# Turning the state-space scans back: two tiles in one set of GpSimd operations

## The chip, the cores and the metric

One core of a Trainium2 chip runs the whole kernel. The metric is the device time of one execution in microseconds (us). The kernel before takes 1242.14 us (median of three runs, 1241.8 to 1242.48). The engines are called PE (TensorE), DVE (VectorE), ACT (ScalarE), POOL (GpSimd) and SP (SyncE, which only issues the transfers here).

## The reference, cut to what matters

Two layers of a decoder trunk on 256 positions of width 1024. Each layer is a gated feed-forward, then four token mixers side by side (stick-breaking attention, an S5 state-space mixer, gated linear attention, dilated attention), gates and an output projection, then a second feed-forward. The change lies in the S5 mixer:

```python
lam_bar = jnp.exp(lam * dt)                                   # complex, one per state
bu = jnp.einsum('bsgh,gph->bsgp', uf.astype(jnp.complex64), b_bar)
def combine(e1, e2):
    a1, b1 = e1
    a2, b2 = e2
    return a1 * a2, a2 * b1 + b2
_, states = lax.associative_scan(combine, (a, bu), axis=1)    # s[t] = lam_bar * s[t-1] + bu[t]
y = jnp.einsum('bsgp,ghp->bsgh', states, c_mat).real + d_skip * uf
```

## The kernel before, in words

PE does all the matrix products in float32r. Every weight block (128 partitions by 2048 columns) is split into a high and a low part, and each product is three matmuls (or a wide one and a correction): ACT writes the high part (`w_hi`, L869), DVE writes the rest (`w_lo`, L1163, two operations of 1024 columns a block). The blocks run through a ring of three slots, filled by SP.

The mixer stage of a layer is a list of 31 blocks, `SEQ`; block number `m` is a projection, a gate or a branch output. Each engine has its own program for the stage, written out by hand: for every `m`, PE multiplies the block and then runs `pieces(m)`; DVE evacuates the block's bank (`evacuate`, L1604; some blocks are evacuated by ACT), splits a later block (`rest_of_weights`, L1163) and then runs its own `pieces(m)`; ACT does the like. Within an engine the order is fixed, and an operation that waits holds up all behind it. Between engines there are only counting semaphores.

The S5 mixer has 1024 complex states, 8 tiles of 128 partitions, handled as four pairs of tiles. The complex recurrence is made real by turning the input by tables of cosines and sines (`rotC`, `rotS`, in tile `G`), scanning with a real decay, and turning the result back. For pair `p`, with `S5_AT = (1, 5, 9, 13)`:

- at m = `S5_AT[p]` PE multiplies the input (`s5_in`), and DVE turns it (`s5_rotate`, L1387 to L1392) into `s5x`;
- at m one later DVE scans (`s5_scan`, L1399, four scans of 256 columns);
- POOL then turns back (`s5_pair`, L1753 to L1766) from `s5x` into `st`: for each of the two tiles six operations of 256 columns: four products, then the two sums. It is all that POOL does at that time. The second to last and last operations of a tile wait for the products, as POOL waits for its own semaphore through `own.link` and `tt` (L1664);
- five blocks after `S5_AT[p]` PE multiplies `st` by the output matrix (`s5_out`, L653). `s5_state` counts one for each tile; its readers wait for the pair's second (L655, L1383, L1597).

Of DVE's other work near it, the change's surroundings hold `rest_of_weights` (L1163: reads `raw` and `w_hi`), the stick-breaking weights of heads 2 and 3 at m = 11 (L1447: reads `attA` and the constant `strict`), and the softmax scores of the dilated attention at m = 16 (L1411 to L1414). At m = 12 PE waits for `sb_w`, which the last L1447 of m = 11 raises, before it multiplies `sbv` by `attA`:

```python
if m == 12:
    pe.wait_ge(s.gla_zread, layer * PER.gla_zread + 1)
    pe.wait_ge(s.sb_w, layer * PER.sb_w + HEADS)
    pe.wait_ge(s.evac_a, layer * PER.evac_a + NTH[SLOT["sbv"]])
    attend(2, sbv, attA).then_inc(s.sb_o, 1)
    gla_scores(1)
```

At m = 20 PE's product waits until DVE has evacuated block 18 (L1604, two blocks before, the same bank).

After the mixers POOL adds the four branches (`mix`, L1768): an operation of 512 columns (L1664 on `attA` or `attB`) and one of 256 (L1773) for each of eight tiles; this part is not changed.

Of the kernel before, what the change touches and what calls it, by code (L numbers as in the profile page):

```python
# [11 lines left out]
ALU = mybir.AluOpType  # L12
AX = mybir.AxisListType

P = 128
LAYERS = 2
T = 256
# [89 lines left out]
class PER:  # L107
# [87 lines left out]
    m_lo = 8  # L195
    dve = 63
    act = 13
    pool = 232


class Signals:
# [29 lines left out]
def build(nc, x_in, stream, params_in, const_in, out):  # L231
    ctx = ExitStack()
    with ctx:
        def sb(name, shape, dt=F32):
            return ctx.enter_context(nc.sbuf_tensor(name, shape, dt))
# [22 lines left out]
        st = sb("st", [P, 2, 2, T])  # L258
# [17 lines left out]
        rotC, rotS = G[:, 2, :, :], G[:, 3, :, :]  # L276
# [30 lines left out]
        s = Signals()  # L307
# [1349 lines left out]
        def _(pool):  # L1657
            pool.memset(attB[:, 0, 0:T], 0.0).then_inc(s.warm, 1)
            pool.wait_ge(s_const, 16)
            for layer in range(LAYERS):  # L1660
                own = Steps(pool, s.pool, layer, PER.pool)

                def tt(o, a, b, op):
                    own.link(pool.tensor_tensor(o, a, b, op))  # L1664
# [88 lines left out]
                def s5_pair(pair):  # L1753
                    x = s5x
                    pool.wait_ge(s.s5_scan, layer * PER.s5_scan + pair + 1)
                    if pair >= 1:
                        pool.wait_ge(s.s5_y, layer * PER.s5_y + pair)
                    for i in range(2):
                        t = 2 * pair + i
                        own.mark(pool.tensor_tensor(x[:, i, 0, 0, :], x[:, i, 1, 0, :], rotC[:, t, :], ALU.mult))  # L1760
                        own.mark(pool.tensor_tensor(x[:, i, 0, 1, :], x[:, i, 1, 1, :], rotC[:, t, :], ALU.mult))
                        re, im = st[:, i, 0, :], st[:, i, 1, :]
                        own.mark(pool.tensor_tensor(re, x[:, i, 1, 1, :], rotS[:, t, :], ALU.mult))
                        own.link(pool.tensor_tensor(im, x[:, i, 1, 0, :], rotS[:, t, :], ALU.mult))
                        tt(re, x[:, i, 0, 0, :], re, ALU.subtract)
                        pool.tensor_tensor(im, x[:, i, 0, 1, :], im, ALU.add).then_inc(s.s5_state, 1)  # L1766

                def mix(dt):  # L1768

# [10 lines left out]
                for pair in range(ST // 2):  # L1780
                    s5_pair(pair)
# [140 lines left out]
```

## Time and profile before

| | |
|---|---|
| Time, median of three | 1242.14 us |
| Time of the profiled execution | 1242.35 us |
| Its span | 1240.6 us |
| PE busy | 1231.1 us (99%) |
| DVE busy | 944.0 us (76%) |
| ACT busy | 677.7 us (55%) |
| POOL busy | 369.1 us (30%) |
| Granted TensorE clock | 1.0 of full speed in the mixer stages |

The span is what lies between the first and the last recorded instruction. Busy is the sum of the recorded durations, overlaps counted once. A recorded duration of a DVE or POOL operation includes the time in which it was issued but held up, so the same operation can show two lengths. Each layer's mixer stage runs from about 205 to 440 us in layer 0 and 614.3 us later in layer 1, with the same pattern.

### The profile page before, as it was taken

What the parts mean: (1) busy time and instruction counts of PE and PEld (TensorE: products, weight loads), DVE (VectorE), ACT (ScalarE), POOL (GpSimd) and SP (SyncE); (2) the same over time, 40 slices, a digit from 0 to 9 for tenths busy, and PEclk for the clock granted to TensorE, in tenths of its full rate; (3) what the DMA queues carried; (4) which work ended last, traced back from release to release, by engine and by line L of the source; (5) the groups of instructions that cost most, each with busy time, mean ns of one, the idle gap of its engine ahead of it and who ended that gap; (6) DMA issues with size and microseconds to landing.
All of it is one profiled execution on the core that took longest, in us unless ns stands there. A gap on an engine that the chain in (4) does not pass through costs nothing.

```text
span 1240.6 us, 23671 instructions
## 1 busy us (share of the span) xinstructions
PE 1231.1 (99%) x9190; PEld 1154.5 (93%) x9190; DVE 944.0 (76%) x1241; ACT 677.7 (55%) x999; POOL 369.1 (30%) x511
## 2 busy tenths in 40 slices
PE   8999999999999999999999999999999999999998
PEld 8999989999999999999999999999999999999998
DVE  6767788889887876666776778788997788666765
ACT  5666645773653554545556655558645445454553
POOL 0088990344404200000001889704443041000000
PEclk9999999999999999999999999999999999999999
DMA  8554554533344465455545454554433445555441
GB/s 333 216 197 160 185 181 179 184 139 134 137 169 172 170 246 193 177 179 193 174 170 199 173 199 173 182 188 170 136 137 137 170 170 204 192 182 190 171 181 68
DMA packets 31605, 220.44 MB, mean 178 GB/s; under 512 B 3633, under 2 KB 3761, under 8 KB 5425
## 3 DMA queue, kind: packets, MB, share of 16 engines
q1 hardware_dynamic: 31536, 219.49, 49.6%
q8 instruction: 48, 0.79, 0.2%
q14 instruction: 21, 0.16, 0.0%
HBM read 218.42 MB, written 1.05 MB: 177 GB/s over the span
## 4 chain that ended last, share of the span: by engine, by line
PE 94%; DVE 3%; ACT 1%; issue 1%; DMA 1%; SPq 0%; DVEq 0%; ACTq 0%
PE banks L520 21%; PE banks L478 20%; PE banks L479 19%; PE banks L480 19%; PE banks L522 10%; PE banks L491 5%; DVE w_lo_t L1163 1%; DVE u_t L1177 1%; DVE hT L1348 1%; ACT w_hi_t L869 1%; DMA raw<-weights 1%; DVE sbqk L1280 0%; DVE sbqk L1278 0%; PE banks L714 0%; DVE w_lo_t L1196 0%
## 5 line engine op out<-in xcount | busy, mean ns | idle before, releaser
L1163 DVE TENSOR_TENSOR w_lo_t<-raw,w_hi_t 128x1024 fp32r<-128x1024 f32 x400 | 507.2, 1308 | 100.1 <-ACT w_hi_t L869 99.6
L869 ACT ACTIVATE w_hi_t<-raw 128x1024 fp32r<-128x1024 f32 x400 | 399.4, 1046 | 115.7 <-PE banks L480 114.4
L478 PE MATMUL banks<-u_t,w_hi_t 128*128 128x256 f32 x944 | 271.5, 288 | 4.1 <-DVE w_lo_t L1196 2.5
L479 PE MATMUL banks<-u_t,w_hi_t 128*128 128x256 f32 x944 | 267.0, 283 | 0.0
L480 PE MATMUL banks<-u_t,w_lo_t 128*128 128x256 f32 x944 | 266.9, 283 | 0.0
L520 PE MATMUL banks<-u_t,w_hi_t 128*128 128x512 f32 x576 | 204.0, 398 | 0.0
L520 PE MATMUL banks<-b_t,w_hi_t 128*128 128x512 f32 x576 | 204.0, 398 | 0.0
L478 PEld LDWEIGHTS banks<-u_t,w_hi_t 128*128 128x128 f32 x944 | 180.8, 191 | 11.5 <-DVE w_lo_t L1196 3.5
L479 PE MATMUL banks<-h_lo_t,w_hi_t 128*128 128x256 f32 x672 | 190.2, 283 | 0.0
L480 PE MATMUL banks<-h_hi_t,w_lo_t 128*128 128x256 f32 x672 | 190.1, 283 | 0.0
L478 PE MATMUL banks<-h_hi_t,w_hi_t 128*128 128x256 f32 x672 | 190.1, 283 | 0.0
L479 PEld LDWEIGHTS banks<-u_t,w_hi_t 128*128 128x128 f32 x944 | 180.9, 192 | 0.1
L480 PEld LDWEIGHTS banks<-u_t,w_lo_t 128*128 128x128 f32 x944 | 180.8, 192 | 0.0
L522 PE MATMUL banks<-u_t,w_lo_t 128*128 128x256 f32 x576 | 161.8, 281 | 0.0
L522 PE MATMUL banks<-b_t,w_lo_t 128*128 128x256 f32 x576 | 161.8, 281 | 0.0
L520 PEld LDWEIGHTS banks<-b_t,w_hi_t 128*128 128x128 f32 x576 | 108.2, 188 | 25.8
L520 PEld LDWEIGHTS banks<-u_t,w_hi_t 128*128 128x128 f32 x576 | 108.2, 188 | 25.8
L478 PEld LDWEIGHTS banks<-h_hi_t,w_hi_t 128*128 128x128 f32 x672 | 128.5, 191 | 1.8
L480 PEld LDWEIGHTS banks<-h_hi_t,w_lo_t 128*128 128x128 f32 x672 | 128.7, 191 | 0.0
L479 PEld LDWEIGHTS banks<-h_lo_t,w_hi_t 128*128 128x128 f32 x672 | 128.6, 191 | 0.0
L924 ACT ACTIVATE sbqk<-sbqk 128x256 f32<-128x256 f32 x88 | 36.8, 418 | 165.6 <-DVE sbqk L1280 120.4
L522 PEld LDWEIGHTS banks<-u_t,w_lo_t 128*128 128x128 f32 x576 | 108.9, 189 | 0.0
(234 smaller groups left out, 1998.0 us busy)
## 6 DMA issues: line engine op xcount, KB each, us to landing
raw<-weights SPq DMA_DIRECT2D x202, 1024.0 KB, 4.9
raw<-weights SPq DMA_DIRECT2D x3, 512.0 KB, 8.3
prm<-params SPq DMA_DIRECT2D x1, 1178.5 KB, 5.3
prm<-params SPq DMA_DIRECT2D x1, 1166.5 KB, 10.1
out_t<-hT SPq DMA_DIRECT2D x4, 256.0 KB, 2.2
cst<-constants SPq DMA_DIRECT2D x1, 896.0 KB, 9.7
hT<-x_t SPq DMA_DIRECT2D x2, 256.0 KB, 3.8
raw<-weights SPq DMA_DIRECT2D x2, 256.0 KB, 4.0
```

Of the source, the lines that this page charges most:

```text
L478: pe.matmul(o, st[0], mv[0], start=start, stop=False, skip_group_check=True)
L479: pe.matmul(o, st[0], mv[1], start=False, stop=False, skip_group_check=True)
L480: ins = pe.matmul(o, st[1], mv[0], start=False, stop=stop, skip_group_check=True)
L491: return pe.matmul(o, st, mv, start=start, stop=stop, skip_group_check=True)
L520: pe.matmul(banks[:, bank + ct, :], st[0], in_t[where][:, :, kt, :], start=kt == 0, stop=False, skip_group_check=True)
L522: ins = pe.matmul(banks[:, bank + ct, 0:T], st[1], in_hi[where][:, kt, :], start=False, stop=kt == KT - 1, skip_group_check=True)
L869: act.activation(w_hi[:, slot, a:a + HALF], raw[:, slot, a:a + HALF], ACT.Copy) \
L924: act.activation(ab[:, buf, 0, :], ab[:, buf, 0, :], ACT.Silu).then_inc(s.h_silu, 1)
L1163: dve.tensor_tensor(w_lo[:, slot, a:a + HALF], raw[:, slot, a:a + HALF], w_hi[:, slot, a:a + HALF].bitcast(F32), ALU.subtract) \
L1177: ins = dve.scalar_tensor_tensor(out=in_lo[where][:, kt, :], in0=hT[:, kt, :], scalar=p_(name)[:, kt:kt + 1], in1=in_hi[where][:, kt, :].b ...
L1348: dve.scalar_tensor_tensor(out=hT[:, 2 * q:2 * q + 2, :].rearrange("p a t -> p (a t)"), in0=banks[:, q, :], scalar=0.5, in1=hT[:, 2 * q:2 ...
```

## The change

POOL turns both tiles of a pair with the same operations. The first one multiplies real and imaginary parts of both tiles by the cosines (1024 columns, the cosine table repeated over the two parts), two of 512 columns multiply by the sines, and two of 512 columns make the sums. The number of own steps that POOL counts falls from 232 to 204. The first sum no longer counts as an own step but raises `s5_state`, and so does the second, so the counter still stands at two more after each pair.

```diff
-    pool = 232
+    pool = 204
...
-                    for i in range(2):
-                        t = 2 * pair + i
-                        own.mark(pool.tensor_tensor(x[:, i, 0, 0, :], x[:, i, 1, 0, :], rotC[:, t, :], ALU.mult))
-                        own.mark(pool.tensor_tensor(x[:, i, 0, 1, :], x[:, i, 1, 1, :], rotC[:, t, :], ALU.mult))
-                        re, im = st[:, i, 0, :], st[:, i, 1, :]
-                        own.mark(pool.tensor_tensor(re, x[:, i, 1, 1, :], rotS[:, t, :], ALU.mult))
-                        own.link(pool.tensor_tensor(im, x[:, i, 1, 0, :], rotS[:, t, :], ALU.mult))
-                        tt(re, x[:, i, 0, 0, :], re, ALU.subtract)
-                        pool.tensor_tensor(im, x[:, i, 0, 1, :], im, ALU.add).then_inc(s.s5_state, 1)
+                    two = slice(2 * pair, 2 * pair + 2)
+                    cos = rotC[:, two, :].unsqueeze(2).to_broadcast([P, 2, 2, T])
+                    sin = rotS[:, two, :]
+                    own.mark(pool.tensor_tensor(x[:, :, 0, :, :], x[:, :, 1, :, :], cos, ALU.mult))
+                    re, im = st[:, :, 0, :], st[:, :, 1, :]
+                    own.mark(pool.tensor_tensor(re, x[:, :, 1, 1, :], sin, ALU.mult))
+                    own.link(pool.tensor_tensor(im, x[:, :, 1, 0, :], sin, ALU.mult))
+                    pool.tensor_tensor(re, x[:, :, 0, 0, :], re, ALU.subtract).then_inc(s.s5_state, 1)
+                    pool.tensor_tensor(im, x[:, :, 0, 1, :], im, ALU.add).then_inc(s.s5_state, 1)
```

## Rows read from the trace of the kernel before

**Rows 1.** The page: busy time of PE and POOL; the chain that ended last, by engine.
```profile
PE 1231.1 (99%) x9190; PEld 1154.5 (93%) x9190; DVE 944.0 (76%) x1241; ACT 677.7 (55%) x999; POOL 369.1 (30%) x511
...
PE 94%; DVE 3%; ACT 1%; issue 1%; DMA 1%; SPq 0%; DVEq 0%; ACTq 0%
```
**Rows 2.** Timeline of POOL in pair 2: start us, us, engine, line, operation.
```profile
282.43 1.71 POOL L1760 TENSOR_TENSOR s5x<-s5x,G 128x256 f32<-128x256 f32 x1 [15.70 <-DVE s5x L1399]
284.10 1.71 POOL L1761 TENSOR_TENSOR s5x<-s5x,G 128x256 f32<-128x256 f32 x1
285.78 1.05 POOL L1763 TENSOR_TENSOR st<-s5x,G 128x256 f32<-128x256 f32 x1
```
**Rows 3.** Timeline of DVE beside it, the two L1163 and L1447 apart.
```profile
282.31 1.23 DVE L1163 TENSOR_TENSOR w_lo_t<-raw,w_hi_t 128x1024 fp32r<-128x1024 f32 x1
283.46 1.76 DVE L1163 TENSOR_TENSOR w_lo_t<-raw,w_hi_t 128x1024 fp32r<-128x1024 f32 x1
285.14 1.09 DVE L1447 SCALAR_TENSOR_TENSOR attA<-attA,cst 128x384 f32<-128x384 f32 x1
286.16 1.09 DVE L1447 SCALAR_TENSOR_TENSOR attA<-attA,cst 128x384 f32<-128x384 f32 x1
```
**Rows 4.** Timeline of PE: end of blocks 10 and 12, start of `pieces(12)`.
```profile
265.75 0.38 PE L478 MATMUL banks<-u_t,w_hi_t 128*128 128x256 f32 x1
271.69 1.06 PE L491 MATMUL banks<-st,s5c 128*32 128x256 f32 x8
...
281.41 0.38 PE L478 MATMUL banks<-u_t,w_hi_t 128*128 128x256 f32 x1
287.35 1.57 PE L491 MATMUL banks<-attA,sbv 128*64 128x256 f32 x16
```
**Rows 5.** POOL in the branch sums (L1768): 512 columns alone and beside L1163.
```profile
374.85 1.29 POOL L1664 TENSOR_TENSOR attA<-attA 128x512 f32<-128x512 f32 x1 [47.94 <-DVE attA L1578]
...
389.81 2.21 POOL L1664 TENSOR_TENSOR attA<-attA 128x512 f32<-128x512 f32 x1 [5.73 <-DVE attA L1578]
```
**Rows 6.** DVE beside the last row of Rows 5.
```profile
389.65 1.22 DVE L1163 TENSOR_TENSOR w_lo_t<-raw,w_hi_t 128x1024 fp32r<-128x1024 f32 x1
390.78 2.32 DVE L1163 TENSOR_TENSOR w_lo_t<-raw,w_hi_t 128x1024 fp32r<-128x1024 f32 x1
```
**Rows 7.** DVE in pair 1, and an unhindered operation of L1447's size.
```profile
249.37 0.56 DVE L1442 TENSOR_TENSOR attA<-attA,cst 128x384 f32<-128x384 f32 x1
...
253.83 3.09 DVE L1163 TENSOR_TENSOR w_lo_t<-raw,w_hi_t 128x1024 fp32r<-128x1024 f32 x2
259.82 3.47 DVE L1163 TENSOR_TENSOR w_lo_t<-raw,w_hi_t 128x1024 fp32r<-128x1024 f32 x2 [2.90 <-ACT w_hi_t L869]
263.22 2.10 DVE L1447 SCALAR_TENSOR_TENSOR attA<-attA,cst 128x384 f32<-128x384 f32 x2
```
**Rows 8.** POOL in pair 1, first and last of twelve.
```profile
253.41 0.74 POOL L1760 TENSOR_TENSOR s5x<-s5x,G 128x256 f32<-128x256 f32 x1 [14.48 <-DVE s5x L1399]
...
265.98 0.74 POOL L1766 TENSOR_TENSOR st<-s5x,st 128x256 f32<-128x256 f32 x1
```
**Rows 9.** POOL's first operation of pair 3; DVE beside and after pair 3.
```profile
314.11 0.74 POOL L1760 TENSOR_TENSOR s5x<-s5x,G 128x256 f32<-128x256 f32 x1 [18.22 <-DVE s5x L1399]
...
319.74 0.69 DVE L1604 SCALAR_TENSOR_TENSOR G<-banks,rstd_row 128x512 f32<-128x512 f32 x1 [1.53 <-PE banks L480]
320.89 3.10 DVE L1163 TENSOR_TENSOR w_lo_t<-raw,w_hi_t 128x1024 fp32r<-128x1024 f32 x2 [0.46 <-ACT w_hi_t L869]
339.36 0.68 DVE L1604 SCALAR_TENSOR_TENSOR G<-banks,rstd_row 128x512 f32<-128x512 f32 x1
```
**Rows 10.** Timeline of PE: the start of block 20.
```profile
340.67 0.36 PE L478 MATMUL banks<-u_t,w_hi_t 128*128 128x256 f32 x1
```
**Rows 11.** Layer 1: L1447's second operation, and PE's `pieces(12)`.
```profile
900.47 1.09 DVE L1447 SCALAR_TENSOR_TENSOR attA<-attA,cst 128x384 f32<-128x384 f32 x1
...
901.66 1.57 PE L491 MATMUL banks<-attA,sbv 128*64 128x256 f32 x16
```

## The prediction

> **What bounds the kernel now.** I read the page first: PE is busy 99% of the span and makes 94% of the chain that ended last; POOL is busy 30% [rows 1]. So a saving on POOL is worth nothing by itself, and the question is what else these operations touch. The list of waits, read next, has nobody waiting for POOL in the state-space part: the only entries of that part are POOL's own waits for DVE's scans, and PE shows no wait for an engine in the blocks after the first few of the stage beyond 0.4 us. What is left is the timelines of POOL and DVE laid side by side, and there both engines have operations of two lengths.
>
> POOL's 256-column operation takes 0.74 us [rows 8] or 1.71 us [rows 2]; the long ones lie beside DVE's split of weights (L1163). DVE's takes 1.23 us or 1.76 us [rows 3], and L1447 takes 1.09 us where an operation of its size takes 0.56 us [rows 3, 7]. In times: POOL's first operation of pair 2 is issued at 282.43 and ends at 284.14, that is 0.60 us after DVE's first L1163 has ended at 283.54; DVE's second is issued at 283.46 and ends at 285.22, 1.08 us after POOL's has ended; POOL's second ends at 285.81, 0.59 us after that [rows 2, 3]. So one of them works while the other stands, a whole instruction at a time, in turns. All DVE operations that show it read two tiles in SBUF; those that read a bank of PSUM and one tile do not.
>
> The Trainium skill has this as a rule: "SBUF — State Buffer", section "Who interferes with whom", says that a DVE instruction with two SBUF inputs and a GpSimd instruction that reads SBUF exclude each other, whoever is first holding the shared port for its whole instruction. By that rule the trace agrees (0.60 and 1.08 us after the other's end), and it speaks against this change, since it makes the holder's instruction longer. By that rule the sum would be the one worked out below; with turns taken within an instruction it would be nothing, the first rival.
>
> **Does the held time grow with the instruction?** The branch sums have a POOL operation of 512 columns: alone it takes 1.29 us, beside L1163 2.21 us [rows 5]. It ends at 392.02, 1.15 us after DVE's first L1163 (390.87), and DVE's second L1163 takes 2.32 us, ending 1.08 us after 392.02 [rows 6]. So POOL holds 0.60 us with 256 columns and 1.15 with 512, which is 0.55 us for each further 256; for 1024 columns I extend the line to 2.25 us. That length stands in no row. From below, it could let DVE in between its rows of 256 and hold no more than 0.60 us at a time; from above, four full operations of 0.74 are 2.96 us. I take 2.25, by the rows of 512.
>
> **The change part by part.** (1) POOL's own time for a pair. Before: twelve holds of 0.60 us, 7.2 us; after: 2.25 + 4 x 1.15 = 6.85 us. With the gaps, the pair gets about 1 to 2 us shorter (before, 253.41 to 266.72 in pair 1 [rows 8]). Nobody waits for it: worth 0. If the pair got longer instead, with every new operation held up as the worst old one (1.71 for 0.74, so 2.3 times some 7.5 us = 17 us), it would still just meet the first PE or DVE use, some 17 us after the start of a pair.
>
> (2) Semaphores: one wait of POOL on itself in a pair goes where there were four; `s5_state` reaches the same count at the last operation. Worth 0; its readers wait for the pair's second count.
>
> (3) What DVE stands for. Each POOL operation now stops a DVE operation for up to 1.15 or 2.25 us where it was 0.55. It costs where DVE is late. I looked for the blocks where DVE has no slack before PE. The tight one is m = 12: DVE's last L1447 ends at 287.25, and PE starts the product that needs it at 287.35, without a wait (block 12 took 5.94 us, as block 10 did) [rows 3, 4]. Slack 0.1 us. From 259.82, where DVE waits for ACT, to there DVE has no idle time, so a delay in it goes through. Layer 1 has the same 0.09 us (901.56 and 901.66) [rows 11].
>
> Pair 2, step by step, with the issue order of before (DVE's L1163 first at 282.31, POOL at 282.43). DVE's first L1163 to 283.54. POOL's 1024 columns: 283.54 + 2.25 = 285.79. DVE's second L1163: + 1.08 = 286.87. POOL's first 512: + 1.15 = 288.02. L1447, first: + 0.42 (as 286.23 from 285.81 in the rows' pattern, 0.56 less what overlaps) = 288.44. POOL's second 512: + 1.15 = 289.59. L1447, second: + 0.42 = 290.01. That is 2.76 us later than 287.25, and PE's `pieces(12)` starts 2.7 us late.
>
> (4) Pair 1 feeds the same chain. POOL starts at 253.41; its 1024 columns end at 255.66, DVE's first L1163 at 256.74, POOL 257.89, DVE 258.97, POOL's third 260.12; DVE's next L1163 (issued 259.82) ends at 261.20, POOL 262.35, DVE 263.43, POOL's fifth 264.58, L1447 265.00 and, now alone, 265.5. Before, they ended at 265.32 [rows 7]. About +0.2 us; pair 0 ends earlier and lets DVE start pair 1 up to 0.4 us earlier. From -0.3 to +0.5; I take 0.
>
> (5) Pair 3 lies beside the softmax of the dilated attention. POOL starts at 314.11 and DVE is 2.2 us late after its first L1163 pair there; the wait for PE before 319.74 (1.53 us) takes up most of it, and L1163 at 320.89 is issued some 0.3 us late [rows 9], just when POOL's third operation ends. If DVE is first, two further holds cost it about 0.5 us more than before; if POOL is first, about 1.7. What hangs on it is the evacuation of block 18, which ends at 340.04 with block 20 waiting for it at 340.67 [rows 9, 10]: slack 0.63. So 0 or about 1.1 us for a layer. DVE is issued some 0.1 us ahead by this count, so I take 0.
>
> (6) PE has no time to give back behind m = 12: what it waits there, the span grows by. Sum: 2 layers x 2.7 = 5.4 us on the profiled execution, whose span of 1240.6 us has 1.75 us around it that stay: 1242.35 + 5.4 = 1247.75. The median before is 0.2 us less than that execution; I say 1247.7.
>
> **The rivals.** *Nothing moves* (0.17): DVE is let in at least between the rows of 256 columns, so it stands for 0.55 us at a time as before, and pair 2 keeps its 287.25. Then POOL's saving is hidden and the time is 1242.1. For it: no row has 1024 columns or a table repeated over a dimension. Against it: the row of 512 with two rows of 256 in it, where DVE stood for 2.32 - 1.23 = 1.09 us.
>
> *Faster* (0.03): fewer holds, and the sum of them in a pair is 0.35 us less, so if POOL's longer operations fell on DVE's PSUM work, L1447 would end earlier. But PE has no wait there now to lose, so it could bring only the tenths of waits elsewhere, at most 1 us in all (1241). That is where it decides: only if the first operation of pair 2 ran clear of L1163.
>
> *More* (0.25): the tie in pair 3 goes to POOL, or the 1024 columns hold 2.96 us: 5.4 + 2 x 1.1 = 7.6, so 1249.9, or 5.4 + 2 x 0.7 = 6.8, so 1249.1.
>
> *Half of it* (0.10): the order at the start of pair 2 shifts by the 0.12 us that separate the two engines, or POOL's 512 columns find L1447's two operations already through, and only the 1024-column hold counts (2.25 - 0.60 = 1.65 us a layer): 1245.4.
>
> **How the numbers follow.** The forecast's own case has 0.45 and gives 1246.8 to 1248.6. The range of 1243.5 to 1250.6 takes in the larger and the half case and leaves out the hidden and the faster one. A measurement of this kernel can tell about 0.2%, 2.5 us, from no change: slower than 1244.6 has 0.45 + 0.25 + 0.10 = 0.80, within it 0.17, faster 0.03.
>
> **What would show it.** In the changed kernel's timeline the second L1163 of pair 2 should take about 3.4 us (1.76 before), L1447's two operations about 1.6 each (1.09), and PE should show a wait for DVE's `attA` at m = 12 of about 2.7 us, twice, at equal places of both layers. POOL's own sum of these lines should fall and its 1024-column operation should last 2.4 us where it runs alone. The rest of PE's waits stays. The forecast is wrong if no DVE operation is longer than the 2.32 us of before, or if DVE's late end at m = 12 is there but PE had slack that the rows hide.

## The result, and the profile after

| | before | changed |
|---|---|---|
| Median | 1242.16 us (4 runs, 1241.8 to 1242.48) | 1253.63 us (4 runs: 1252.35, 1252.41, 1254.86, 1255.11) |
| Profiled execution | 1242.35 us, span 1240.6 | 1252.41 us, span 1250.6 |
| Mean granted TensorE clock | 1.0 | 0.997 (0.994 to 0.995 in the two longer runs) |

The ratio of changed to before is 1.0091, with a 95% interval of 1.0079 to 1.0103: slower by 11.5 us, where 5.5 were forecast. The direction was right, the forecast size was half of what came, and the time lies outside the range.

The page, busy times and the chain by engine:

```profile
PE 1235.6 (99%) x9190; PEld 1158.5 (93%) x9190; DVE 964.4 (77%) x1241; ACT 677.5 (54%) x999; POOL 354.8 (28%) x455
...
PE 91%; DVE 5%; ACT 1%; issue 1%; DMA 1%; SPq 0%; ACTq 0%; DVEq 0%
```

Against [rows 1] POOL does its work in 14.3 us less, DVE is busy 20.4 us longer with the same instructions, and DVE has 5% of the chain. The groups of instructions say where: L1163 of DVE grew from a mean of 1308 to 1363 ns, L1447 from 1090 to 1360.

```profile
L1163 DVE TENSOR_TENSOR w_lo_t<-raw,w_hi_t 128x1024 fp32r<-128x1024 f32 x400 | 529.0, 1363 | 91.4 <-ACT w_hi_t L869 90.8
L1447 DVE SCALAR_TENSOR_TENSOR attA<-attA,cst 128x384 f32<-128x384 f32 x8 | 10.6, 1360 | 0.0
```

Pair 2 of layer 0, POOL's timeline (start, us):

```profile
282.36 3.41 POOL L1761 TENSOR_TENSOR s5x<-s5x,G 128x1024 f32<-128x1024 f32 x1 [17.96 <-DVE s5x L1399]
285.74 2.25 POOL L1763 TENSOR_TENSOR st<-s5x,G 128x512 f32<-128x512 f32 x1
287.95 1.58 POOL L1764 TENSOR_TENSOR st<-s5x,G 128x512 f32<-128x512 f32 x1
```

and DVE's beside it:

```profile
282.28 1.23 DVE L1163 TENSOR_TENSOR w_lo_t<-raw,w_hi_t 128x1024 fp32r<-128x1024 f32 x1
283.43 3.43 DVE L1163 TENSOR_TENSOR w_lo_t<-raw,w_hi_t 128x1024 fp32r<-128x1024 f32 x1
286.78 1.63 DVE L1447 SCALAR_TENSOR_TENSOR attA<-attA,cst 128x384 f32<-128x384 f32 x1
288.33 1.63 DVE L1447 SCALAR_TENSOR_TENSOR attA<-attA,cst 128x384 f32<-128x384 f32 x1
```

These answer to [rows 2] and [rows 3]. The two engines take turns, and each of POOL's turns has grown: its 1024 columns end 2.26 us after DVE's first L1163 (283.51 to 285.77), its 512 columns 1.13 us after the second (286.86 to 287.99). The second L1447 ends at 289.96, where before it ended at 287.25.

PE's timeline at m = 12 in layers 0 and 1, then at m = 17 in layer 0 (a number in brackets is PE's idle time ahead of the row):

```profile
290.06 1.63 PE L491 MATMUL banks<-attA,sbv 128*64 128x256 f32 x16 [2.67 <-issue]
...
910.87 1.54 PE L491 MATMUL banks<-attA,sbv 128*64 128x256 f32 x16 [2.66 <-issue]
...
332.18 1.64 PE L491 MATMUL banks<-dqk 64*128 64x128 f32 x8
```

The last row holds the matmuls of two heads and took 0.94 us before. It is longer because those of the second head start only at 332.93, after DVE's second L1414 has ended at 332.79.

The stretches after the first of these waits, each with its length, then PE's busy time, PEld, DVE, ACT, POOL, granted clock, DMA share and GB/s:

```profile
288.00:290.00 2.00, 0.00 (x0) 0.00 (x0) 2.00 (x3) 1.49 (x2) 1.92 (x2) 1.00 0.87 287
290.00:292.00 2.00, 1.95 (x24) 1.59 (x25) 2.00 (x2) 0.28 (x1) 2.00 (x2) 0.84 0.56 234
292.00:294.00 2.00, 2.00 (x46) 2.00 (x44) 2.00 (x2) 0.32 (x1) 1.29 (x1) 0.50 0.00 0
294.00:296.00 2.00, 2.00 (x28) 1.94 (x29) 0.98 (x3) 0.00 (x0) 0.00 (x0) 0.50 0.36 70
296.00:298.00 2.00, 2.00 (x11) 2.00 (x11) 2.00 (x5) 0.00 (x0) 0.00 (x0) 0.50 0.84 324
298.00:300.00 2.00, 2.00 (x18) 2.00 (x18) 1.83 (x6) 0.00 (x0) 0.00 (x0) 0.95 0.33 139
```

Here is what the forecast lacked. PE stands still through 288 to 290, works again from 290.06, and is then granted 0.50 of its clock (the 1.2 GHz level) from about 291.4 to 298.2. It looks busy, but block 13 comes late: the multiplication for pair 3 (`s5_in(3)`) starts at 302.45 where it was 296.71, and 3.03 of those 5.74 us arose after PE had resumed.

Following marks of PE's program through both profiles (start of the same group of matmuls, changed less before) gives the whole account in us; a row is what was added there:

| | layer 0 | layer 1 |
|---|---|---|
| m = 12, PE waits for L1447 | 2.73 | 2.73 |
| behind it, half clock | 3.03 | none (-0.04) |
| m = 17, PE waits for L1414 | 0.70 | 0.84 |
| all else in the layer | 0.0 | 0.0 |

The sum is 10.0, the growth of the span. The two longer executions took some 2.5 to 2.7 us more at a mean clock of 0.994 to 0.995. That fits a second stretch at half clock in layer 1, or a longer one in layer 0; they left no trace.

### The profile page after: what moved, and what is told of

Same layout as the page of the kernel before. It is cut to its first block, busy times and chain, and to the rows that moved or that the text cites. A ratio compares the mean times of both kernels' runs of the same rounds, so it can differ in the third digit from the quotient of the medians.

```text
span 1250.6 us, 23615 instructions
## 1 busy us (share of the span) xinstructions
PE 1235.6 (99%) x9190; PEld 1158.5 (93%) x9190; DVE 964.4 (77%) x1241; ACT 677.5 (54%) x999; POOL 354.8 (28%) x455
## 4 chain that ended last, share of the span: by engine, by line
PE 91%; DVE 5%; ACT 1%; issue 1%; DMA 1%; SPq 0%; ACTq 0%; DVEq 0%
PE banks L520 20%; PE banks L478 19%; PE banks L479 18%; PE banks L480 18%; PE banks L522 10%; PE banks L491 5%; DVE w_lo_t L1163 2%; ACT w_hi_t L869 1%; DVE u_t L1177 1%; DVE hT L1348 1%; DMA raw<-weights 1%; DVE sbqk L1280 0%; DVE sbqk L1278 0%; PE banks L714 0%; DVE w_lo_t L1196 0%
## 5 line engine op out<-in xcount | busy, mean ns | idle before, releaser
L1163 DVE TENSOR_TENSOR w_lo_t<-raw,w_hi_t 128x1024 fp32r<-128x1024 f32 x400 | 529.0, 1363 | 91.4 <-ACT w_hi_t L869 90.8
L478 PEld LDWEIGHTS banks<-u_t,w_hi_t 128*128 128x128 f32 x944 | 181.4, 192 | 11.5 <-DVE w_lo_t L1196 3.5
```

Of the source, the lines that this page charges most:

```text
L478: pe.matmul(o, st[0], mv[0], start=start, stop=False, skip_group_check=True)
L1163: dve.tensor_tensor(w_lo[:, slot, a:a + HALF], raw[:, slot, a:a + HALF], w_hi[:, slot, a:a + HALF].bitcast(F32), ALU.subtract) \
```

## The experiments

The theory before the experiments: POOL holds DVE off for a whole instruction; it costs time only where a late DVE operation is one that PE waits for; and the idle PE sometimes gets the lower clock afterwards. The rival: the wide form costs by itself, spread over the stage. The "before" of these runs had medians of 1242.3 to 1242.4 us.

**Wide in pair 2 alone, and wide in all but pair 2.** `s5_pair` chooses the form by pair:

```diff
+                    if pair in (2,):        # the other kernel: (0, 1, 3)
                         ...                 # the change's five operations
+                    else:
+                        ...                 # the twelve of before
```

> Only pair 2 of each layer is turned back in the wide form (one operation of 1024 columns, four of 512); pairs 0, 1 and 3 keep the twelve of 256. Theory (GpSimd holds DVE off for a whole instruction, and it matters only where DVE has no slack before PE, at m = 12; the idle PE then gets a lower clock for some 7 us in some executions): PE waits 2.7 us at m = 12 of each layer and not at m = 17, 1242.2 + 5.4 = 1247.6 us, and 3 us more for each layer in which the clock falls (up to 1253.6). Rival (the cost comes with each wide pair alike): a quarter of the change's 11.5 us, 1245.0 us, with waits spread over the stage.

Measured: 1249.18 us (1248.05 to 1249.94), ratio 1.0057 (1.0040 to 1.0074). In the profile, at clock 1.000, PE waits 2.66 us at m = 12 in each layer, its marks move by 2.73 there, and nothing is lost at m = 17:

```profile
290.65 1.11 PE L491 MATMUL banks<-attA,sbv 128*64 128x256 f32 x10 [2.66 <-issue]
```

The profiled execution took 1248.05 us; the two at a clock of 0.997 took 1249.9.

> Pairs 0, 1 and 3 wide, pair 2 in the old form. Theory: no wait of PE at m = 12, only the 0.7 to 0.8 us at m = 17 that pair 3 makes, in each layer: 1243.7 us, and the clock stays at 1.0. Rival (each wide pair costs alike): three quarters of 11.5 us, 1250.8 us.

Measured: 1243.0 us, ratio 1.0005 (0.9996 to 1.0015), clock 1.0. PE's marks move by 0.00 at m = 12 and by 0.42 and 0.43 at m = 17, less than the 0.7 to 0.8 that I expected: here DVE's L1163 of pair 3 was issued at 320.59, just ahead of POOL at 320.68, and its two operations took 3.45 us, where they took 3.81 in the change. One wide pair of four thus carries almost all of the loss, and three carry 0.7 us. The rival, that each costs alike, is out.

**The 1024 columns cut in two of 512.**

```diff
-                    cos = rotC[:, two, :].unsqueeze(2).to_broadcast([P, 2, 2, T])
                     ...
-                    own.mark(pool.tensor_tensor(x[:, :, 0, :, :], x[:, :, 1, :, :], cos, ALU.mult))
+                    for part in range(2):
+                        own.mark(pool.tensor_tensor(x[:, :, 0, part, :], x[:, :, 1, part, :], rotC[:, two, :], ALU.mult))
```

> The change with its operation of 1024 columns cut in two of 512 (real part of both tiles, imaginary part of both tiles), six operations a pair. Theory (held for the whole instruction, 1.15 us for 512 columns, 2.25 for 1024): DVE's second L1163 of pair 2 takes 2.3 us in place of 3.4, but one more GpSimd operation then comes ahead of L1447; its second ends 1.1 us earlier than in the change, PE waits 1.6 us at m = 12: about 1246.5 us, with up to 3 us a layer more if so short a wait also brings the clock down. Rival (the wide form as such is slow, or the clock falls whatever the wait's length): as the change, 1252 to 1254 us.

Measured: 1247.16 us (1247.05 to 1247.42), ratio 1.0039 (1.0025 to 1.0053), clock 1.0 in all five runs. PE's wait at m = 12:

```profile
288.59 1.54 PE L491 MATMUL banks<-attA,sbv 128*64 128x256 f32 x16 [1.57 <-issue]
```

The wait is 1.57 us, as counted in holds; at m = 17 the marks move by 0.96 us a layer. No clock was lost. With shorter instructions the cost falls to less than half of the change's 11.5 us: what costs is how long each instruction is.

**The 1024 columns third, not first.**

```diff
-                    own.mark(pool.tensor_tensor(x[:, :, 0, :, :], x[:, :, 1, :, :], cos, ALU.mult))
                     re, im = st[:, :, 0, :], st[:, :, 1, :]
                     own.mark(pool.tensor_tensor(re, x[:, :, 1, 1, :], sin, ALU.mult))
-                    own.link(pool.tensor_tensor(im, x[:, :, 1, 0, :], sin, ALU.mult))
+                    own.mark(pool.tensor_tensor(im, x[:, :, 1, 0, :], sin, ALU.mult))
+                    own.link(pool.tensor_tensor(x[:, :, 0, :, :], x[:, :, 1, :, :], cos, ALU.mult))
```

> The change with its operation of 1024 columns third among the five in place of first. Theory (what counts is the sum of the three holds that come before the second L1447, not their order or the longest): the second L1447 of m = 11 ends within 0.1 us of where the change has it, 289.96 in its profile, and PE waits 2.7 us at m = 12: 1251 to 1254 us with the clock. Rival (the first long hold is what does it): PE waits less than 2 us there.

Measured: 1250.54 us (1249.16 to 1250.7), ratio 1.0062 (1.0044 to 1.0080). DVE in pair 2:

```profile
282.11 3.46 DVE L1163 TENSOR_TENSOR w_lo_t<-raw,w_hi_t 128x1024 fp32r<-128x1024 f32 x2
285.49 4.28 DVE L1447 SCALAR_TENSOR_TENSOR attA<-attA,cst 128x384 f32<-128x384 f32 x2
```

L1163 is 1.1 us better off than in the change (3.46 for two, there 4.57) and L1447 1.1 us worse (4.28, there 3.18); they end at 289.77, in a profile whose marks all come 0.2 us earlier. PE waits 2.66 us. The sum of the holds ahead of the second L1447 decides, not their order. The total is a little below what I expected, since less clock was lost: 1.54 us in layer 0 behind the wait and none in layer 1.

**DVE does the two L1447 before the L1163 of block 11.** The change otherwise.

```diff
+                        if m in (11,):
+                            pieces(m)
                         rest_of_weights(layer, k0 + m // RING + 1, m % RING)
                         ...
-                        pieces(m)
+                        if m not in (11,):
+                            pieces(m)
```

> The change, and DVE does its pieces of m = 11 (the two L1447) before the L1163 of that block instead of after it; the same operations. Theory: the two L1447 then end before 286 us, PE does not wait at m = 12 and its clock stays at 1.0; left is the wait at m = 17 of 0.7 to 0.8 us a layer: 1243.7 us. Rival (the loss is contention all over, or the clock falls for another cause): 1250 us or more.

Measured: 1245.08 us (ten runs, 1244.76 to 1245.38), ratio 1.0022 (1.0012 to 1.0031), clock 1.0 in all. DVE and POOL at m = 11, and PE at m = 12:

```profile
281.67 1.00 DVE L1447 SCALAR_TENSOR_TENSOR attA<-attA,cst 128x384 f32<-128x384 f32 x2
282.58 2.35 DVE L1163 TENSOR_TENSOR w_lo_t<-raw,w_hi_t 128x1024 fp32r<-128x1024 f32 x2
```
```profile
281.83 5.37 POOL L1764 TENSOR_TENSOR s5x<-s5x,G 128x1024 f32<-128x1024 f32 x1 [17.96 <-DVE s5x L1399]
```
```profile
286.79 1.57 PE L491 MATMUL banks<-attA,sbv 128*64 128x256 f32 x16
```

The wait at m = 12 and the lost clock are gone, as the theory had it. (POOL's 1024-column operation stood 5.37 us this time. It ends at 287.20, 2.27 us after DVE's second L1163 at 284.93, and none of the four DVE operations is longer than alone: DVE did not let it in between them, so the turns are not strict; why POOL lost each time here and not in pair 2 of the change stays open.) But m = 17 now costs 1.43 us a layer, not 0.8. It is the tie that the prediction named, falling to POOL: its fourth operation of pair 3 is issued at 320.25, DVE's L1163 at 320.33, and the two L1163 take 4.54 us. What PE then waits for:

```profile
326.19 0.89 PE L491 MATMUL banks<-dqk 64*128 64x128 f32 x4 [0.24 <-DVE dmx L1414]
327.37 0.89 PE L491 MATMUL banks<-dqk 64*128 64x128 f32 x4 [0.28 <-DVE dmx L1414]
```

**The same at m = 16 as well:** `if m in (11, 16)`, so that L1411 to L1414 go ahead of the block's L1163.

> The change, with DVE's pieces ahead of its L1163 in two blocks: m = 11 (the two L1447) and m = 16 (the scores of the dilated attention, L1411 to L1414). Theory (the loss is made of DVE operations that PE waits for and that stand behind a held-up L1163): the wait at m = 17 goes too; left is the 0.3 us a layer at the start of block 17 that the kernel with the first reorder alone showed: 1242.8 us. Rival (part of the loss is contention without a place): 1244.5 us or more.

Measured: 1241.46 us (ten runs), ratio 0.9993 (0.9983 to 1.0002). The waits at m = 17 are gone: the second L1414 ends at 323.57, PE needs it at 326.86. The 0.3 us that I expected to stay did not: it had been PE's wait for the first L1414, seen in the lines just above, not one at the start of block 17. Instead PE starts the transposes of the two heads behind block 20 (L714) earlier, against its place behind block 19, by 0.29 us for the first and another 0.08 for the second in layer 0, and 0.27 and 0.08 in layer 1; the kernel before had also been waiting there.

**A late L1447 without any change on POOL.** The kernel before, with sums over a parameter tile put ahead of L1447 on DVE:

```diff
+                    if m == 11:
+                        for i, n in enumerate((1024, 1024, 256)):   # the other kernel: four of 1024
+                            dve.tensor_reduce(idle[:, i:i + 1], prm[:, 0:n], AX.X, ALU.add)
```

> The kernel before, with three more operations on DVE at m = 11 ahead of the two L1447: sums over 1024, 1024 and 256 columns of one tile into a scratch tile, together some 2.6 us; GpSimd as before. Theory (any lateness of L1447 is a wait of PE, and the wait alone can bring the clock down): PE waits 2.6 us at m = 12 in each layer, 1247.5 us, and in some executions up to 3 us a layer more. Rival (the lower clock comes from GpSimd's long operations): 1247.5 us in all executions, clock 1.0.

Measured: 1249.18 us median of five: 1247.71, 1247.98, 1249.18, 1255.28, 1255.7, at mean clocks of 0.999, 0.999, 0.997, 0.991, 0.991; ratio 1.0078 (1.0048 to 1.0108). In the profiled execution (1247.71) PE's marks move by 2.19 us at m = 12 of both layers, less than the 2.6 put in, since POOL's operations passed meanwhile; layer 1 loses 1.56 us more to the clock, layer 0 none. PE's wait in layer 1, and the clock around it (columns as above, the granted clock third from the end):

```profile
905.62 1.87 PE L492 MATMUL banks<-attA,sbv 128*64 128x256 f32 x10 [2.12 <-issue]
```
```profile
903.00:905.60 2.60, 0.50 (x5) 0.30 (x4) 2.60 (x5) 2.00 (x2) 2.44 (x4) 1.00 0.90 372
905.60:907.00 1.40, 1.38 (x10) 1.18 (x12) 1.40 (x2) 0.00 (x0) 1.40 (x2) 0.56 0.02 6
907.00:909.00 2.00, 2.00 (x25) 1.44 (x22) 1.92 (x2) 0.60 (x1) 2.00 (x2) 0.50 0.00 0
909.00:911.00 2.00, 2.00 (x59) 1.96 (x56) 0.18 (x1) 0.00 (x0) 1.90 (x3) 0.95 0.56 90
```

With POOL as before, the clock falls, and by different amounts from run to run. So the long GpSimd operations are not needed to bring it down. Nor do they bring it down alone: the kernels above that have them, but a wait of 1.57 us or none at m = 12, kept a mean clock of 0.999 to 1.0.

> As the last, with four sums of 1024 columns, some 4.5 us. Theory (a longer wait brings the clock down more surely): PE waits 4.5 us in each layer, 1251.2 us, and the clock falls in both layers in most executions, 3 us each: 1257 us. Rival (clock falls from something else): 1251.2 us.

Measured: 1259.96 us (1259.74 to 1260.51), ratio 1.0141 (1.0123 to 1.0159), clock 0.991 to 0.992 in all four. The clock in layer 0 (columns as above):

```profile
288.00:292.00 4.00, 0.15 (x2) 0.18 (x4) 4.00 (x5) 1.67 (x2) 3.92 (x6) 0.76 0.41 174
292.00:296.00 4.00, 4.00 (x44) 3.08 (x44) 3.15 (x3) 0.60 (x1) 3.58 (x3) 0.50 0.00 0
296.00:300.00 4.00, 4.00 (x52) 3.94 (x51) 1.59 (x4) 0.00 (x0) 0.00 (x0) 0.50 0.76 266
300.00:304.00 4.00, 4.00 (x22) 4.00 (x21) 3.83 (x9) 0.00 (x0) 0.00 (x0) 0.53 0.00 0
304.00:308.00 4.00, 4.00 (x34) 3.49 (x33) 1.12 (x3) 1.26 (x2) 0.00 (x0) 1.00 0.00 0
```

PE's marks moved by 4.36 us at m = 12 in each layer, and by 5.36 and 4.19 us more behind it at half clock, more than the 3 I gave it. The clock fell here while PE still stood: at about 290.1, and PE started again at 291.85.

**Does the wide form gain anything once its cost is gone?** Both kernels with both reorders, beside each other on one chip.

> The kernel before, its GpSimd operations as they were, with DVE's pieces ahead of its L1163 at m = 11 and m = 16. Theory (the 0.3 us a layer that PE no longer waited at m = 20 and 21 in the change with both reorders came from the reorder at m = 16, not from GpSimd's wide form): 1241.6 us, 0.7 us less than before, and equal to the change with both reorders. Rival (the wide form has a gain of its own once its cost is gone): this stays at 1242.3 and the other is faster.

Measured: 1241.53 us (11 runs, 1240.9 to 1242.15), ratio 0.9994 (0.9985 to 1.0003).

> The change with both reorders once more, for a closer interval beside the last kernel: 1241.5 us, 0.7 us less than before; the same as the last by the theory, 0.7 us faster than it by the rival.

Measured: 1241.34 us (11 runs, 1240.46 to 1241.89), ratio 0.9993 (0.9984 to 1.0002). The medians of the two lie 0.2 us apart, well inside their scatter. So the wide form is worth nothing here even at its best. Both medians are 0.8 to 1.0 us under the before measured beside them, in three comparisons now, but each interval just reaches 1: a gain of that size is likely and not proved.

## Why the prediction was right in direction and wrong in size

*The held time grows with the instruction (0.60, 1.15, 2.25 us).* Right: 1.13 for 512 columns and 2.26 for 1024 in pair 2. That POOL holds DVE off to the end of its instruction also where one input is a table repeated over a dimension was taken from the rows of 512, and the rival in which DVE gets in between rows of 256 fell with the 3.43 us of the second L1163 (3.41 forecast).

*Step 3, pair 2.* Right: the second L1447 was to end at 290.01 and ended at 289.96; PE was to wait 2.7 us a layer and its marks moved 2.73. The cut of the 1024 columns, the reordered products and the reorder on DVE each moved that wait to where the sum of holds puts it. What the last one showed besides is that "in turns" is a pattern of these rows, not a rule: there POOL waited for four DVE operations in a row.

*Step 4, pair 1.* I took 0 from -0.3 to +0.5; PE's marks between m = 5 and m = 11 did not move (0.0 in all the kernels).

*Step 5, pair 3.* Both the order and the place were wrong. DVE was not late at its L1163 (on PE's marks it lies where it did before, 5.74 us on, where 0.3 us of lateness was forecast), but it was not first either: POOL's fourth operation was under way.

```profile
326.63 1.57 DVE L1163 TENSOR_TENSOR w_lo_t<-raw,w_hi_t 128x1024 fp32r<-128x1024 f32 x1 [0.46 <-ACT w_hi_t L869]
328.12 2.31 DVE L1163 TENSOR_TENSOR w_lo_t<-raw,w_hi_t 128x1024 fp32r<-128x1024 f32 x1
```
```profile
325.83 1.28 POOL L1765 TENSOR_TENSOR st<-s5x,st 128x512 f32<-128x512 f32 x1
327.08 2.27 POOL L1766 TENSOR_TENSOR st<-s5x,st 128x512 f32<-128x512 f32 x1
```

So the two L1163 took 3.81 us where they took 3.10, 0.7 us more, between the 0.5 that I counted for DVE first and the 1.7 for POOL first; the experiments show both ends (3.45 and 4.54 us, 0.42 and 1.43 us lost). As to the place, I let the lateness reach the evacuation of block 18 with its 0.63 us of slack, and passed over `dsa_scores(3)` at m = 17, in front of which there was none. In the profile of before, which I did not weigh there, the second L1414 ends at 326.35, and PE starts the two heads' matmuls, of which the second head's need it, at 326.44.

```profile
325.94 0.41 DVE L1414 TENSOR_REDUCE dmx<-attB 128x1 f32<-128x256 f32 x1
```

So the term was 0.70 and 0.84 us in place of 0; this is 1.5 of the 4.6 us by which the profiled execution missed the forecast's 5.4.

*Step 6, "what it waits there, the span grows by".* This is the step that failed. The waits alone, with the two at m = 17, come to 1242.16 + 5.46 + 1.54 = 1249.2 us, inside the range. The step left out that PE works at half clock for a while after such a wait: 3.03 us in layer 0 of the profiled execution, a larger term than the wait itself (2.73). The kernel with delayed L1447 shows the same with POOL unchanged (1.56 us behind a wait of 2.19, and 5.36 and 4.19 behind waits of 4.36), and the kernel with the 1.57 us waits shows none in five runs. The loss varies from run to run of one kernel, so a single profile gives no fixed price. I had read the clock of before, 1.0 throughout, and did not ask what the wait that I forecast would do to it. By the runs there are now, an estimate of 0 to 4.5 us for each of the two waits belonged there, and a range up to about 1257: the longest execution with the delayed L1447 took 13.4 us more than before, of which its waits are 4.4, so that some 9 us are left for two places.

The Trainium skill, "TensorE: Matmul & The Clock Gate", section "Part 1: The HAM clock gate (the "warmup" mystery)", says that TensorE's clock is set by how busy the engine has been recently. The traces agree: in the mixer stages 0.50 was granted only around the waits. The same section says that how many matmuls run at the lower clock at the start of a kernel varies between runs of one kernel. The runs here show such a variation in the middle of one: 1247.71 to 1255.7 us for one kernel.

*Chances.* Slower by over 0.2% had 0.8 and came; the range ended at 1250.6, for want of the clock. The rival *More* (1249.1 to 1249.9) lies near the 1249.2 us of the waits alone, but by other terms: no hold of 2.96 us is in the rows, and pair 3 cost 0.70 and 0.84 us a layer, not 1.1.

What stays open: why the clock falls after a wait of 2.7 us in one layer and not in the other of the same execution; by what rule the engines take turns; and whether the longer runs of the change had it in both layers, since no trace was taken of them.

## What to carry to other kernels

Fewer, wider GpSimd instructions are no gain where nobody waits for GpSimd, and they lengthen each time that a VectorE operation with two SBUF inputs is held off: lay the two timelines side by side, find the VectorE operations whose end stands within a fraction of a microsecond of TensorE's start, and count the holds up to them. Look at every such place to the end of the stage; the one passed over here cost 1.5 us. And where a forecast makes TensorE stand idle, add a term for its clock behind the wait, with a range from nothing to more than the wait itself.

## What the runs showed of the hardware

- Two engines that exclude each other: a VectorE operation of 1024 columns with two SBUF inputs took 1.22 us alone, and 1.76, 2.32 or 3.43 us behind a GpSimd operation of 256, 512 or 1024 columns: the held time is 0.55 to 0.60, 1.1 and 2.2 us.
- The loser of the race can lose several times: GpSimd's 1024 columns, 2.4 us alone, took 5.37 us beside four VectorE operations issued back to back, none of which was held up.
- Where TensorE had stood still for 2.1 to 2.7 us (two places in each of four profiled executions), it was granted 0.50 of its clock in three of the eight places, for 3.4, 3.4 and 6.8 us. A wait of 1.57 us brought no loss in either place, waits of 4.3 us one in both, for 13.7 and 10.2 us (4.2 to 5.4 us lost).
- The clock did not fall at a fixed distance from the wait: between 1.7 us before TensorE started again and 1.3 us after.
